# The RMS norm ahead of the attention block, applied behind its products

## The reference, cut to what matters

```python
def rms_norm(x, g):
    y = x32 * lax.rsqrt(jnp.mean(x32 * x32, axis=-1, keepdims=True) + RMS_EPS)
    return (y * g.astype(jnp.float32)).astype(x.dtype)

def first_block(...):                 # two layers: S5 + SwiGLU, short conv + SwiGLU
    ...
        x = x + g2 * swiglu(h, w_ffn_in[i], w_ffn_out[i])
    return rms_norm(x, final_g)

def dilated_attention_mixer(x, w_in, w_out):
    proj = (x @ w_in).reshape(B, S, 3, 3, 16, 64)
    for g, (window, dilation) in enumerate(((128, 1), (512, 4), (2048, 16))):
        q = rotary(proj[:, :, g, 0], pos)
        k = rotary(proj[:, :, g, 1], pos)
        o, lse = dilated_window_attention(q, k, proj[:, :, g, 2], window, dilation)
    ...
def second_block(x, ...):
    y = dilated_attention_mixer(x, ...)
    x = layer_norm(DEEPNORM_ALPHA * x + y, ...)      # the normed x is also the residual
```

## Time and profile before

| | us |
|---|---|
| median of 3 runs | 2630.32 |
| lowest, highest | 2629.37, 2632.2 |
| the profiled execution's time | 2631.51 |
| its span in the profile | 2629.7 |
| PE busy | 2584.1 (98%) |
| DVE busy | 1438.2 (55%) |
| ACT busy | 1050.4 (40%) |

### The profile page before, as it was taken

The page is one execution under the profiler, slowest core; times in us unless marked ns, Lnnn a source line. Parts: engine busy times, 40 slices in busy tenths (PEclk is TensorE's granted clock), DMA queues, the critical chain, the costliest instruction groups (busy, mean ns, idle before and its releaser), DMA issues.

```text
span 2629.7 us, 38280 instructions
## 1 busy us (share of the span) xinstructions
PE 2584.1 (98%) x15944; PEld 2190.6 (83%) x15944; DVE 1438.2 (55%) x2165; ACT 1050.4 (40%) x1560; POOL 120.2 (5%) x147
## 2 busy tenths in 40 slices
PE   6999999999999999999999999999999999999998
PEld 3789888888898888888888888988888988988887
DVE  8676555565463333365555555844336767834335
ACT  4734222233242222255555555533223564522323
POOL 6810000000000000000000000000000000000000
PEclk8999999999999999999999999999999999999999
DMA  7583555423322222322222222132222122222220
GB/s 259 90 325 129 192 192 192 184 73 97 112 97 96 96 96 98 110 74 73 73 76 82 73 80 86 54 128 96 96 96 81 55 91 90 104 96 96 96 96 33
DMA packets 55241, 286.89 MB, mean 109 GB/s; under 512 B 7154, under 2 KB 17666, under 8 KB 29091
## 3 DMA queue, kind: packets, MB, share of 16 engines
q1 hardware_dynamic: 49106, 241.98, 27.6%
q0 software_dynamic: 5968, 42.52, 4.3%
HBM read 278.19 MB, written 2.10 MB: 107 GB/s over the span
## 4 chain that ended last, share of the span: by engine, by line
PE 90%; DVE 5%; ACT 2%; DMA 1%; issue 1%; SPq 1%; POOL 0%; ACTq 0%; DVEq 0%
PE PS L728 18%; PE PS L729 18%; PE PS L730 18%; PE PS L862 4%; PE PS L864 4%; PE PS L863 4%; PE PS L821 1%; PE PS L820 1%; PE PS L819 1%; PE PS L891 1%; PE PS L892 1%; PE PS L893 1%; PE PS L948 1%; PE PS L754 1%; PE PS L755 1%; PE PS L756 1%
## 5 line engine op out<-in xcount | busy, mean ns | idle before, releaser
L728 PE MATMUL PS<-Hl,Wh 128*128 128x512 f32 x1256 | 489.0, 389 | 0.8 <-DVE Wl L1762 0.7
L729 PE MATMUL PS<-Hh,Wl 128*128 128x512 f32 x1256 | 488.7, 389 | 0.0
L730 PE MATMUL PS<-Hh,Wh 128*128 128x512 f32 x1256 | 488.6, 389 | 0.0
L1270 ACT CAST Wh<-raw 128x2048 fp32r<-128x2048 f32 (+2 forms) x152 | 273.8, 1846 | 403.1 <-PE PS L730 380.7
L1762 DVE TENSOR_TENSOR Wl<-raw,Wh 128x2048 fp32r<-128x2048 f32 (+1 forms) x158 | 342.5, 2207 | 63.7 <-ACT Wh L1270 62.9
L729 PE MATMUL PS<-Gh,Wl 128*128 128x512 f32 x848 | 329.9, 389 | 0.0
L730 PE MATMUL PS<-Gh,Wh 128*128 128x512 f32 x848 | 329.9, 389 | 0.0
L728 PE MATMUL PS<-Gl,Wh 128*128 128x512 f32 x848 | 329.9, 389 | 0.0
L728 PEld LDWEIGHTS PS<-Hl,Wh 128*128 128x128 f32 x1256 | 235.7, 188 | 50.4 <-DVE Wl L1762 1.4
L730 PEld LDWEIGHTS PS<-Hh,Wh 128*128 128x128 f32 x1256 | 235.7, 188 | 48.9
L729 PEld LDWEIGHTS PS<-Hh,Wl 128*128 128x128 f32 x1256 | 235.7, 188 | 48.8
(11 more groups left out here) (490 smaller groups left out, 4702.1 us busy)
## 6 DMA issues: line engine op xcount, KB each, us to landing
raw<-wstream SPq DMA_DIRECT2D x152, 1024.0 KB, 6.2
raw<-wstream SPq DMA_DIRECT2D x64, 768.0 KB, 4.5
adab<-adaw POOLq DMA_DIRECT2D x28, 1024.0 KB, 5.3
adah<-adaw POOLq DMA_DIRECT2D x12, 1024.0 KB, 7.1
raw<-wstream SPq DMA_DIRECT2D x20, 512.0 KB, 3.8
raw<-adap SPq DMA_DIRECT2D x4, 1024.0 KB, 10.7
ada_land<-adap SPq DMA_DIRECT2D x4, 1024.0 KB, 18.9
MT<-KPX SPq DMA_DIRECT2D x64, 64.0 KB, 2.8
```

The source lines that it names most:

```text
L728: mm(o, Wh[:, s, c0:c0 + P], xl[:, k, :], start=k == 0, stop=False)
L729: mm(o, Wl[:, s, c0:c0 + P], xh[:, k, :], start=False, stop=False)
L730: last = mm(o, Wh[:, s, c0:c0 + P], xh[:, k, :], start=False, stop=k == kt - 1)
L1270: nc.scalar.copy(w_high(p, h, widths[h]), raw[:, h, 0:widths[h]]).then_inc(split_h, 1)
```

## The change

- Pair 47 is made as pair 46 is: whole tiles of 512 tokens, no halves, and no `norm_sums` within.
- New, on ACT and DVE, `scaled_input`: as soon as an X tile is finished, ACT writes `Hh` = X times the norm's weight vector (by class), DVE writes `Hl`, ACT squares, DVE adds the square. No 1/rms is needed for this. X is not changed. The split of pair 48 stands behind the tiles 0 to 3 on both engines, where it stood ahead of the squares.
- PE makes tile 0 of unit 0 alone, k by k, then `attn_square_sums`: one float32 matmul of 512 columns (mean squares in every partition, for the tables) and ten with one column (mean squares of 128 tokens each, one per partition, for the value rows). Then the tiles 1 to 8, dense.
- DVE then makes 1/rms over 512 columns into PSUM bank 6, multiplies both rotary tables by it, and makes the ten-column version `RK`. ACT's value copies take their scale from `RK`: per unit four of 256 columns and six of 128, where there were two of 512, one of 512 and one of 256.
- X itself is normed during unit 0 (`normed_input`, two tiles behind each of the rotary steps 2 to 5); it is needed as the residual after the attention.

The first `scaled_input` below is ACT's, the second DVE's; `if n == 1` stands in ACT's `attn_swap`.

```diff
-                        if d == 1 and ci == 2:
+                        if d == 1 and ci == 2 and n == 1:
                             last_product(p, n + 1, tiles)
...
+            def attn_square_sums():
+                pe.wait_ge(nm_sa, square_adds_done(4, KT - 1, 0))
+                mm(PS[:, 4, :], ones_d, SQA, start=True, stop=True)
+                for r in range(4):
+                    mm(PS[:, 5, r:r + 1], SQA.rearrange("p (n r) -> p r n", r=4)[:, r, :], ones_d[:, 0:1], start=True, stop=True)
+                for w, n0 in enumerate((0, 64, 32)):
+                    for f in range(2):
+                        j, c0 = 4 + 2 * w + f, 256 * f + 2 * n0
+                        last = mm(PS[:, 5, j:j + 1], nv[:, 0, c0:c0 + P], ones_d[:, 0:1], start=True, stop=True)
+                last.then_inc(nm_mm, 2)
...
-                    for h in range(2):
-                        for k in range(KT):
-                            if h == 0 and k == 4:
-                                norm_sums(4, 1)
-                            pe.wait_ge(nm_l, normed_done(4, k, h))
-                            for m in range(3):
-                                last = attn_k_half(m, k, h)
...
-                    for i in range(3, 9):
+                    for k in range(KT):
+                        pe.wait_ge(nm_l, normed_done(4, k, 0))
+                        last = attn_k(P_ATTN, 0, attn_bank(0, 0), k)
+                    last.then_inc(acc_ready, 1)
+                    attn_square_sums()
+                    for i in range(1, 9):
                         attn_dense(0, i)
...
+            def scaled_input():
+
+                def tile(k):
+                    act.wait_ge(nm_x, tiles_done(4, k, 0))
+                    A(by_class(Hh[:, k, :]), X[:, k, :].rearrange("p (n r) -> p n r", r=4), ACT.Copy, scale=NRM[:, 4, k:k + 1]).then_inc(nm_h, 2)
+                    squares(4, (k,))
+
+                ahead(P_ATTN - 2)
+                act.sem_inc(free_act, 1)
+                nc.scalar.preload_act_table_set("natural_log_exp_and_others")
+                for k in range(4):
+                    tile(k)
+                down_pair(P_ATTN - 1)
+                for k in range(4, KT):
+                    tile(k)
+                split_half(P_ATTN + 1, 0)
+                act.wait_ge(nm_v, 1 + halves_done(4, 0))
+                o.link(A(nv[:, 1, :], nv[:, 2, :], ACT.Ln))
+                A(Rn[:, :], nv[:, 1, :], ACT.Exp, scale=-0.5).then_inc(nm_r0, 1)
+                act.wait_ge(nm_v, 1 + halves_done(4, 1))
+                o.link(A(sq[:, 0, 16:26], sq[:, 0, 0:10], ACT.Ln))
+                A(RK[:, :], sq[:, 0, 16:26], ACT.Exp, scale=-0.5).then_inc(nm_r0, 1)
+                split_half(P_ATTN + 1, 1)
...
+                if n == 1:
+                    act.wait_ge(at_s["rk"], 1)
...
-                nc.scalar.copy(V12[:, 2 * i - 14:2 * i - 12, :].rearrange("p r e -> p (r e)"), PS[:, attn_bank(un, i), :]).then_inc(at_s["v"], 1)
+                for x in range(2):
+                    r = 2 * i - 14 + x
+                    ins = A(V12[:, r, :], PS[:, attn_bank(un, i), 256 * x:256 * x + 256], ACT.Copy, scale=RK[:, r:r + 1])
+                ins.then_inc(at_s["v"], 1)
...
-                    nc.scalar.copy(V0[:, lo:hi, :].rearrange("p j e -> p (j e)"), PS[:, attn_bank(un, i), 0:(hi - lo) * P]).then_inc(at_s["v0"], 1)
+                    for j in range(lo, hi):
+                        ins = A(V0[:, j, :], PS[:, attn_bank(un, i), (j - lo) * P:(j - lo) * P + P], ACT.Copy, scale=RK[:, 4 + j:5 + j])
+                    ins.then_inc(at_s["v0"], 1)
...
+            def scaled_input(add):
+
+                def tile(k):
+                    hh = Hh[:, k, :].bitcast(F32)
+                    dve.wait_ge(nm_h, normed_done(4, k, 0))
+                    STT(by_class(Hl[:, k, :]), X[:, k, :].rearrange("p (n r) -> p n r", r=4), NRM[:, 4, k:k + 1], by_class(hh),
+                        ALU.mult, ALU.subtract).then_inc(nm_l, 2)
+                    if k:
+                        dve.wait_ge(nm_sq, squares_done(4, k, 0))
+                        if k > 1:
+                            dve.wait_ge(nm_sa, square_adds_done(4, k - 1, 0))
+                        TT(SQA, SQA, sq[:, k % 2, :], ALU.add).then_inc(nm_sa, 1)
+
+                p = P_ATTN - 2
+                ahead(p)
+                for k in range(4):
+                    dve.wait_ge(acc_ready, 4 * p + k + 1)
+                    add(k, PS[:, 4 * (p % 2) + k, :], slice(0, T)).then_inc(nm_x, 1)
+                dve.wait_ge(nm_x, tiles_done(4, 3, 0))
+                dve.sem_inc(free_dve, 1)
+                for k in range(4):
+                    tile(k)
+                p = P_ATTN - 1
+                ahead(p)
+                for k in range(4, KT):
+                    dve.wait_ge(acc_ready, 4 * p + k - 3)
+                    add(k, PS[:, 4 * (p % 2) + k - 4, :], slice(0, T)).then_inc(nm_x, 2)
+                    if k == KT - 1:
+                        dve.wait_ge(nm_x, tiles_done(4, k, 0))
+                        dve.sem_inc(free_dve, 1)
+                    tile(k)
+                dve.wait_ge(nm_sa, square_adds_done(4, KT - 1, 0) - 3)
+                for f in range(2):
+                    ins = V_.tensor_copy(by_block(nv[:, 0, :], f), SQA.rearrange("p (b n f r) -> p f r b n", b=4, n=32, f=2, r=2)[:, f])
+                    ins.then_inc(nm_sa, 1 + f)
+                dve.wait_ge(nm_mm, 8 + halves_done(4, 1))
+                TS(nv[:, 2, :], PS[:, 4, :], RMS_EPS, None, ALU.add).then_inc(nm_v, 1)
+                TS(sq[:, 0, 0:10], PS[:, 5, 0:10], RMS_EPS, None, ALU.add).then_inc(nm_v, 1)
+                low_half(P_ATTN + 1, 0)
+                dve.wait_ge(nm_r0, 1 + halves_done(4, 0))
+                link(TT(nv[:, 0, :], Rn[:, :], Rn[:, :], ALU.mult))
+                link(STT(nv[:, 0, :], nv[:, 0, :], -0.5, nv[:, 2, :], ALU.mult, ALU.mult))
+                link(STT(PS[:, 6, :], nv[:, 0, :], 1.5, Rn[:, :], ALU.add, ALU.mult))
+                dve.wait_ge(late_in, 16 * 6)
+                for x in range(2):
+                    step(TT(by_class(ROT[:, x, :]), by_class(ROT[:, x, :]), PS[:, 6, :].rearrange("p (n r) -> p n r", r=4), ALU.mult))
+                dve.wait_ge(nm_r0, 1 + halves_done(4, 1))
+                newton(RK[:, :], sq[:, 0, 0:10], sq[:, 0, 16:26], sq[:, 0, 16:26])
+                dve.sem_inc(at_s["rk"], 1)
+                low_half(P_ATTN + 1, 1)
+
+            def normed_input(k):
+                STT(X[:, k, :], X[:, k, :], NRM[:, 4, k:k + 1], PS[:, 6, :], ALU.mult, ALU.mult).then_inc(nm_t, 2)
...
+                    if un == 0 and 3 <= i < 7:
+                        normed_input(2 * i - 6)
+                        normed_input(2 * i - 5)
```

More of the change, by code:

```diff
@@ L92, in tiles_done @@
     before = 0 if n == 1 else 10 + 12 * (n - 2)
+    if n == 4 and k >= f:
+        return before + f + 2 * (k - f + 1)
     return before + (k + 1 if k < f else f + h * (KT - f) + k - f + 1)
@@ L103, in square_adds_done @@
     before = 0 if n == 1 else 8 + 10 * (n - 2)
+    if n == 4:
+        return before + (k if k < KT - 1 else 10)
     return before + (k if k < f else f - 1 + h * (KT - f) + k - f + 1)
@@ L111, in normed_done, with half_tiles_before @@
 def normed_done(n, k, h):
+    if n == 4:
+        return 16 * (n - 1) + 2 * (k + 1)
     return 16 * (n - 1) + 8 * h + k + 1
+def half_tiles_before(n):
+    return 2 * (n - 1 if n < 5 else n - 2)
 def norm_bank(n, h):
@@ L362, in build @@
             "o",
-            "otl")}
+            "otl",
+            "rk")}
         def by_block(a, f):
@@ L1254, in squares @@
                         act.wait_ge(nm_sa, square_adds_done(n, k - 2, h))
-                    A(SQA if n and k == 0 else sq[:, k % 2, c], X[:, k, c], ACT.Square).then_inc(nm_sq, 1)
+                    A(SQA if n and k == 0 else sq[:, k % 2, c], X[:, k, c], ACT.Square).then_inc(nm_sq, 2 if n == 4 and k >= 4 else 1)
             def rsqrt_estimate(n, h):
@@ L1319, in norm @@
                 normed(n, 0, (4, 5), shift)
-                if n == 4:
-                    split_half(P_ATTN + 1, 0)
-                    rsqrt_estimate(n, 1)
-                    normed(n, 0, (6, 7), shift)
-                    split_half(P_ATTN + 1, 1)
-                else:
-                    normed(n, 0, (6, 7), shift)
-                    if n == 8:
-                        act.wait_ge(nm_mean, 2 * LN_INDEX[8] + 2)
-                        A(mu[:, half(1)], PS[:, norm_bank(8, 1) + 1, half(1)], ACT.Square).then_inc(nm_m2, 1)
-                    rsqrt_estimate(n, 1)
+                normed(n, 0, (6, 7), shift)
+                if n == 8:
+                    act.wait_ge(nm_mean, 2 * LN_INDEX[8] + 2)
+                    A(mu[:, half(1)], PS[:, norm_bank(8, 1) + 1, half(1)], ACT.Square).then_inc(nm_m2, 1)
+                rsqrt_estimate(n, 1)
                 if n in SECOND:
@@ L1559, in _ @@
             swiglu(P_FFN_B)
-            norm(4)
+            scaled_input()
             def attn_swap(un, i):
```

(14 more changed lines are left out.)

42 lines of the change are left out of this document (6 added, 36 removed).

## The result

The changed kernel takes 2634.89 us (median of 22 runs, lowest 2632.61), the kernel before 2631.2 us over 22 runs beside it (2629.37 to 2634.45). The ratio is 1.0014, with an interval of 1.0007 to 1.0020: 3.7 us slower, and within the 0.2% that the prediction called "same". The time was forecast as 2630.8, in a range up to 2633.8; it lies 1.1 us above the range.

The account below looks back on a forecast made before the run. PE, under way in 98% of the span, was taken as the bound. Tile 3 starting 3.55 us earlier at full clock, against 4.0 us lost at half clock, gave +0.45 on 2630.32: 2630.8 us, range 2626.0 to 2633.8.

Parts of the forecast that it names:

- taken off for a fall within the sums: Half-clock loss in the sums and tile 1, 4.75 us, was counted as 4.0 because the fall may begin within the sums.
- base, 3 runs against 22: Time of the kernel before from which the forecast started: 2630.32 us, to which +0.45 us was added.
- Case A: The forecast itself: PE waits of about 4 us, the clock falls, +0.45 us, 2630.8 us; chance 0.55.
- DVE and ACT up to the last `Hl`: Unit 0's X tiles: tiles 4 to 7 take 3.55 us each in series; last `Hl` ends at 1128.95, PE waits 3.25 us.
- the loss by half clock: Around the sums and tile 1: PE falls to half clock, costing 3.15 plus 1.6 us, taken as 4.0.
- rival D: Clock stays low longer into the tiles; at 6.4 us of low stretch +2.8 us, 2633.1 us; chance 0.12.
- PE's sums: One 512-column and ten one-column float32 matmuls after tile 0: 3.15 us at full clock, 6.3 at half.
- rival B: No fall of PE's clock around the sums: -3.55 us, 2626.8 us; chance 0.2.
- the cover of the value copies: ACT's ten value copies per unit instead of four: at most 1 us more, hidden in all 8 units.
- the cover of tile 3: Tile 3 waits for pair 49's second low half, but tiles 1 and 2 (10.88 us) cover it, with 1.7 us left.
- C: `Hl` on DVE at plain cost and no fall of the clock: -6.75 us, 2623.6 us; chance 0.07.
- E: PE's waits not shorter than before, `Hl` at 1.5 us adding 2.8 us to the forecast: 2633.6 us; chance 0.06.

## Why the prediction was right and wrong

The miss is 2634.89 - 2630.8 = 4.1 us. By its steps:

| step | forecast | measured | again | adds |
|---|---|---|---|---|
| start of the sums after pair 47's start | 25.87 | 26.80 | 26.76 | 0.93 |
| sums, whole at half clock | 6.3 | 6.00 | 6.11 | -0.3 |
| taken off for a fall within the sums | 0.75 | none | none | 0.75 |
| tiles 1 and 2, with their loss by half clock | 10.88 + 1.6 = 12.48 | 13.20 | 12.53 | 0.72 |
| value copies, unit 7 | 0 | 0.8 | 0.8 | 0.8 |
| other | 0 | about 0.3 | | 0.3 |
| base, 3 runs against 22 | 2630.32 | 2631.2 | | 0.9 |

The column "again" is the second profile of the changed kernel; the last column goes by the first. The steps that failed are DVE's wait for `Hh`, sized 0.3 us too short in each of four tiles; the half-clock loss, from which 0.75 us were taken off and which was longer in the tiles; and the cover of unit 7's value copies, a term put at nothing. A base of three runs did the rest.

- **Right: the mechanism.** Case A's waits of some 4 us came (3.8, as 1.05 and 2.78 at the last two k of tile 0, and none at the sums); the clock fell; the gain of the missing halves was given back. The surcharge of the `Hl` form was right (1.15 forecast, 1.187 measured), the table products too (1.1 and 1.086), pair 48's low part as well (done 10.7 us after pair 47's start, as forecast).
- **Mis-sized: DVE and ACT up to the last `Hl`.** It ended 25.30 us after pair 47's start, not 24.3. The term is DVE's wait for `Hh`, taken as 1.1 and measured as 1.42, four times over; each tile takes 3.82 instead of 3.55. Of the 0.3 about half is ACT's row, 1.22 instead of the 1.08 that came from doubling the surcharge of the earlier trace rows; the rest is the time from DVE's add to ACT's start and from ACT's end to DVE's start, 0.09 + 0.10, for which the sum had next to nothing. Of the 0.9 us wait at the sums nothing showed: the last three matmuls of tile 0 ran at half clock, 1.45 us instead of 0.68, and hid it.
- **Mis-sized: the loss by half clock.** The prediction added up 3.15 us in the sums and 1.6 on tile 1, and then took 0.75 off, in case the fall came within the sums. It came before them in both profiles, so there was nothing to take off. In the first profile tiles 1 and 2 were at half clock for 4.75 us and lost 2.32; in the second they lost 1.65, as forecast. The longer stretch is a mild form of rival D, which began to lose once the low stretch in the tiles passed 0.8 us; that a profile shows it and the next does not was outside any of the cases.
- **Right at half clock, wrong at full: PE's sums.** At half clock the 6.3 us were 6.00 and 6.11. At full clock the forecast of 3.15 was 3.96 in the run with DVE one tile behind: the prediction scaled all ten by the clock, which holds for the six contiguous ones (0.22 and 0.43), while the four strided ones take 0.415 at either level. The 0.8 us between them would have counted in rival B, where the clock holds; in the changed kernel it cost nothing. The Trainium skill, SBUF — State Buffer, section Door 1: The DMA port swizzle, has a penalty for accesses that move on to another 16-byte line each time. With double time for the four, a factor that was the prediction's own, the sums were to be 0.9 us longer by it; the runs show 0.8 at full clock and none at half.
- **Missed: the cover of the value copies.** "Hidden, in all 8 units" was argued from the border of units 0 and 1 and carried over to all. There it holds: the exponentials still waited 0.22 us for DVE, and PE waits for nothing from there to unit 7 (1182 to 1620 us). But unit 7 has another successor, the output product, whose wait for the pair stands right behind the copies. A cover argued for one border is not one for the last round of a loop.
- **Right: the cover of tile 3.** Pair 49's second low half ended at about 1144.3, tile 3 started at 1148.36, and PE waited for nothing. The loads moved on SP's queue delayed nobody.
- **Rivals.** B (no fall) was refuted by the clock column. C: `Hl` was not at plain cost. E's total (2633.6) was passed, but not by its mechanism, since `Hl` took 1.19 and not 1.5. What none of them had is the kernel that would have made the change pay: the waits were a matter of order on DVE's queue. The prediction's own line "in series, since DVE's queue puts the next add behind the square" stated the cause, and I took it as given.
- **The range.** Its upper end lay 3.0 us above the forecast, and these misses add up to 4.1, nearly all with the same sign. Even without the 0.9 of the base the time would have lain just above it.

## What to carry to other kernels

Where one engine's output is finished by two others in turn, let the second run one tile behind the first: here that alone ended 3.8 us of waits and took 5.7 us off the time. Small matmuls in a row were bad for PE twice here, for their own time and for the clock of the dense work behind them; put singly between dense matmuls they cost only themselves. And when a reordering gives nothing, read the clock column on both sides of it: here 10 us, 0.8 of them in unit 7, lay under two thin stretches, and each of them, left alone, still brought the clock down.
